# The second products of an MLP by one level of Strassen's scheme, on one Trainium2 core

## What is computed

```python
hm = rms_norm(x, g_mlp[l])
x = x + jnp.square(jax.nn.relu(hm @ w_up[l])) @ w_down[l]   # w_up 1024 x 4096, w_down 4096 x 1024
return rms_norm(x, g_final)
```

## Time and profile before

| | |
|---|---|
| median of 3 runs (lowest, highest) | 1576.56 us (1574.56, 1578.52) |
| the profiled execution | 1579.46 us |
| its span in the trace | 1577.7 us |
| busy: PE, DVE, ACT, POOL | 1531.7, 890.2, 715.3, 223.5 us |
| the MLP, from about 1219 us to the end | about 358 us |

### The profile page before, as it was taken

The page is one execution under the profiler, slowest core; times in us unless marked ns, Lnnn a source line. Parts: engine busy times, 40 slices in busy tenths (PEclk is TensorE's granted clock), DMA queues, the critical chain, the costliest instruction groups (busy, mean ns, idle before and its releaser), DMA issues.

```text
span 1577.7 us, 19176 instructions
## 1 busy us (share of the span) xinstructions
PE 1531.7 (97%) x7086; PEld 1239.6 (79%) x7086; DVE 890.2 (56%) x1753; ACT 715.3 (45%) x1630; POOL 223.5 (14%) x194
## 2 busy tenths in 40 slices
PE   7998999999999999999899999999999999999998
PEld 5886777877898777777587878788777888888886
DVE  6467485657565566666457557664455444434344
ACT  6553343334355667665335354442344433324243
POOL 3203020202120003122022005220001100000001
PEclk9999999999999999999999999999999999999999
DMA  6522121323424221112133312134323333333332
GB/s 194 161 68 80 54 80 55 107 68 120 119 76 147 77 61 56 54 56 67 41 121 94 94 55 67 56 109 131 93 81 94 94 93 96 105 94 93 97 103 81
DMA packets 88636, 141.56 MB, mean 90 GB/s; under 512 B 6368, under 2 KB 36448, under 8 KB 88544
## 3 DMA queue, kind: packets, MB, share of 16 engines
q1 hardware_dynamic: 87824, 139.55, 29.3%
q10 hardware_dynamic: 720, 0.80, 0.2%
HBM read 138.23 MB, written 2.10 MB: 89 GB/s over the span
## 4 chain that ended last, share of the span: by engine, by line
PE 79%; DVE 8%; ACT 5%; issue 3%; POOL 3%; DMA 2%; SPq 0%; ACTq 0%; POOLq 0%; DVEq 0%
PE banks L1259 12%; PE banks L1261 12%; PE banks L1260 12%; PE banks L1264 10%; PE banks L1266 10%; PE banks L1265 10%; PE banks L1222 3%; DVE sb_w_split L1964 3%; ACT sb_junk L1529 2%; DVE sb_arena L1973 2%; PE banks L1437 1%; PE banks L1384 1%; ACT sb_w_split L1561 1%; PE banks L1500 1%; DVE sb_arena L1964 1%
## 5 line engine op out<-in xcount | busy, mean ns | idle before, releaser
L1964 DVE TENSOR_TENSOR sb_w_split<-sb_raw,sb_w_split 128x512 fp32r<-128x512 f32 (+4 forms) x530 | 345.0, 693 | 365.9 <-ACT sb_w_split L1561 365.5
L1561 ACT ACTIVATE sb_w_split<-sb_raw 128x512 fp32r<-128x512 f32 (+4 forms) x530 | 288.1, 592 | 411.2 <-PE banks L1261 192.0
L1259 PE MATMUL banks<-sb_actA,sb_w_split 128*128 128x512 f32 x672 | 277.1, 412 | 2.8 <-DVE sb_arena L1964 2.5
L1261 PE MATMUL banks<-sb_actA,sb_w_split 128*128 128x512 f32 x672 | 263.0, 391 | 0.0
L1260 PE MATMUL banks<-sb_actA,sb_w_split 128*128 128x512 f32 x672 | 262.1, 390 | 0.0
L1264 PE MATMUL banks<-sb_w_split,sb_actB 128*128 128x512 f32 (+2 forms) x464 | 181.4, 391 | 1.6 <-DVE sb_w_split L1964 1.6
L1266 PE MATMUL banks<-sb_w_split,sb_actB 128*128 128x512 f32 (+2 forms) x464 | 175.9, 379 | 0.0
L1265 PE MATMUL banks<-sb_w_split,sb_actB 128*128 128x512 f32 (+2 forms) x464 | 175.5, 378 | 0.0
L1264 PE MATMUL banks<-sb_w_split,sb_actA 128*128 128x512 f32 (+1 forms) x384 | 154.4, 402 | 13.5 <-DVE sb_w_split L1964 9.6
L1259 PEld LDWEIGHTS banks<-sb_actA,sb_w_split 128*128 128x128 f32 x672 | 126.5, 188 | 32.7 <-issue 7.1
L1266 PE MATMUL banks<-sb_w_split,sb_actA 128*128 128x512 f32 (+1 forms) x384 | 150.3, 391 | 0.0
(11 more groups left out here) (226 smaller groups left out, 2188.2 us busy)
## 6 DMA issues: line engine op xcount, KB each, us to landing
sb_raw<-in_a_w_in SPq DMA_DIRECT2D x66, 256.0 KB, 3.0
sb_raw<-in_w_up SPq DMA_DIRECT2D x32, 512.0 KB, 3.8
sb_raw<-in_w_down SPq DMA_DIRECT2D x32, 512.0 KB, 3.8
sb_raw<-in_w_in SPq DMA_DIRECT2D x24, 512.0 KB, 3.7
sb_raw<-in_mem_w_kv SPq DMA_DIRECT2D x16, 512.0 KB, 3.8
sb_raw<-in_w_ckv SPq DMA_DIRECT2D x16, 512.0 KB, 3.8
sb_raw<-in_a_w_in SPq DMA_DIRECT2D x15, 512.0 KB, 3.7
sb_raw<-in_a_w_out SPq DMA_DIRECT2D x12, 512.0 KB, 3.9
```

The lines of the kernel that those rows point to most:

```text
L1259: pe.op.matmul(out, hi[:, cs], x.hi(k), start=i == 0, stop=False)
L1261: t = pe.op.matmul(out, lo[:, cs], x.hi(k), start=False, stop=last_i)
L1561: act.op.activation(hi[:, cs], raw[:, cs], ACT.Copy).then_inc(act.mark(m("w_hi"), 2 * n + part + 1), 1)
L1964: dve.op.tensor_tensor(out, a, b, op).then_inc(dve.mark(*mark) if mark else dve.tick(), 1)
```

## The change

It replaces `dn{b}0` and `dn{b}1` of each block by seven products `wn{b}{i}` of quarter size: 512 of contraction, 256 tokens (two tiles), 512 output columns. Write the squared activations of a block as a 2 x 2 matrix of blocks f00, f01, f10, f11 (token half, feature half) and the weights as W00, W01, W10, W11. In the order of execution (`WINO_ORDER`) they are:

| product | left | weight | goes to |
|---|---|---|---|
| P1 | f00 | W00 | x, and a running sum |
| P2 | f01 | W10 | x |
| Q5 | S1 = f10 - f11 | W00 + W01 | x, twice |
| Q7 | f10 - f00 | W01 + W11 | x, twice |
| P6 | S2 = f00 - S1 | W00 + W01 + W11 | the running sum |
| Q3 | f01 - S2 | W11 | x |
| N4 | -f11 | W00 + W01 + W11 + W10 | x |

- **Weights.** The four quarters of a block (1 MB each) are loaded whole by SP (`fetchR`), two into the arena and two into `x_res`, which is free by then. The sums are made in place by DMAs that POOL issues with `accum_op=ALU.add` (`tsum`, 512 KB each, eight in a block), each after the split of the chunk that it changes. Chunks of `wn` are split from there by one ACT and one DVE instruction of 128x1024 each. A chunk of `wn` is 12 matmuls.
- **Activations.** ACT squares each tile into `f_plain`; `s1` and `ssum` make the differences on DVE; `g` makes the high part (ACT) and the low part (DVE) of each left operand, 128x512 at a time, two for each product. The relu buffer has two tiles in place of eight. `up{b}0` and `up{b}1` now take two tiles of each feature half, loaded as two DMAs of 256 KB a chunk.
- **Norm scale.** It is applied before the square: DVE's eviction of `up` is max(., 0) times `row["e"]`, which `nrow` makes (four transposes on PE, a copy on ACT). `esum` and `r2` are gone.
- **Results.** Products with two destinations are added by two DVE operations a tile; 20 a block in place of 8. After the last block `fix` adds the running sum onto three quarters of x (six DVE operations), and token tiles 0 and 1 are closed after Q3, tiles 2 and 3 after N4.
- **Banks.** The MLP rotates through all eight PSUM banks, except in the up products of block 0.

The core of the diff:

```diff
-        for half in range(2):
-            add(f"dn{b}{half}", ("w_down",), D_MODEL, [(half * 512, 512)], "token", f"f{b}", "tok", k0=b * D_MODEL)
+        for i in range(7):
+            add(f"wn{b}{i}", None, 512, [(0, 512)], "token", f"F{b}{i}", "wn" if len(LANDS[i]) == 1 else "wn2",
+                tokens=SEQ // 2)
...
+        p.soon.extend([[("g", b, P1, 0), ("g", b, P2, 0)], [("s1", b, 0)], [("g", b, Q5, 0)], [("ssum", b, 3, 0), ("g", b, N4, 0)],
+                       [("g", b, Q7, 0)], [("ssum", b, 2, 0)], [("g", b, P6, 0), ("ssum", b, 4, 0)], [("g", b, Q3, 0)]])
+        p.product(f"up{b}1", into=banks(4) if b else (0, 1, 2, 3),
+                  tail=lambda j: [("relu", b, up_tile(1, j))] + ([("g", b, P1, 1)] if j == 1 else []))
...
+        work = {P1: [[("g", b, P2, 1), ("tsum", b, Q5, 0)], [("s1", b, 1), ("g", b, Q5, 1), ("tsum", b, Q5, 1)]],
+                P2: [[("tsum", b, P6, 0)], [("ssum", b, 3, 1), ("tsum", b, P6, 1)]],
+                Q5: [[("g", b, Q7, 1)], [("ssum", b, 2, 1)]], Q7: [[("g", b, P6, 1)], [("ssum", b, 4, 1)]],
+                P6: [[("g", b, Q3, 1), ("tsum", b, N4, 0)], [("g", b, N4, 1), ("tsum", b, N4, 1)]], Q3: [], N4: []}
...
+        if b == 3:
+            work[Q3] = [[("fix", 0)], [("fix", 1)], [("fix", 2)],
+                        [(kind, *([1] if kind == "fsq" else []), j) for j in (2, 3) for kind in ("fsq", "fg")]]
...
             if is_wino(name):
+                dve.wait_ge(m("w_hi"), 2 * n + 2)
+                dve.op.tensor_tensor(lo, raw, hi.bitcast(F32), ALU.subtract
+                                     ).then_inc(dve.mark(m("w_lo"), 2 * n + 2), 2)
+                continue
...
+        elif kind == "tsum":
...
+            pool.op.dma_start(v.wino_weight(i, c), v.io["w_down"][r0:r0 + 256, c0:c0 + 512].rearrange("(k p) n -> p k n", p=P),
+                              accum_op=ALU.add).then_inc(m(f"dma_sum{i}{c}"), 16)
```

More of the change, by code:

```diff
@@ L408, in need, with product @@
                 self.force(step)
-    def product(self, name, before_ev=(), soon=None, into=None, first=True, tail=None):
+    def product(self, name, before_ev=(), soon=None, into=None, first=True, tail=None, whole=False):
         pr = PRODUCTS[name]
@@ L415, in product @@
         ks, i, n_j = k_tiles(name), 0, n_out(name)
-        spans = [(c,) for c in range(len(pr.order))] if tail is None else [(0,), tuple(range(1, len(pr.order)))]
+        spans = [tuple(range(len(pr.order)))] if whole else [(c,) for c in range(len(pr.order))]
         for span in spans:
@@ L778, in order_of_work @@
     p.put(("load_g",))
-    p.side(0, [("sqp", "e", 7)], lag=0)
-    p.side(0, (), ("nsq", "e"), ("esum",), lag=4000)
+    scales(0, "e", after=[("sqp", "e", 7)])
     for j in range(TT):
         for g in range(2):
-            p.side(0, (), ("xt", j, g))
-    for b in range(4):
[L785 to L789, removed]
+            p.side(0, (), ("xt", j, g), lag=1300)
@@ L997, in __init__ @@
         at = Layout(self.arena)
-        self.out_sb = at.take(TT, D_MODEL)
-        self.relu, self.sq = at.take(KD, SEQ), at.take(2, SEQ)
+        at.at = 4096
+        flat = self.x_res[:, :, :].rearrange("p a b -> p (a b)")
+        first = Layout(self.arena).take(2, 4 * 512)
+        self.w_quarter = [w.rearrange("p (k n) -> p k n", k=4) for w in
+                          (first[:, 0, :], first[:, 1, :], flat[:, 0:2048], flat[:, 2048:4096])]
+        self.f_plain, self.relu = at.take(KD, SEQ), at.take(2, SEQ)
         at.at = 9280
         self.x_tok, self.g_row = at.take(TT, D_MODEL), at.take(D_MODEL)
+        self.out_tile = [a[:, i, :] for a in (flat[:, 0:2048].rearrange("p (a b) -> p a b", a=2),
+                                              first[:, 1, :].rearrange("p (a b) -> p a b", a=2)) for i in range(2)]
+        self.first_sum = at.take(2, 512)
+        at.at = 19520
+        self.s_plain = at.take(2, 512)
+        self.row["e"] = at.take(SEQ)
         def squares_at(ring, total, n=2):
@@ L1174, in raw_total, with wino_split @@
     def raw_total(self, n):
-        return 16 * sum(len(PRODUCTS[self.plan.chunks[m][0]].parts) for m in range(n % RAW_SLOTS, n + 1, RAW_SLOTS))
+        return 16 * sum(len(PRODUCTS[self.plan.chunks[m][0]].parts) for m in range(n % RAW_SLOTS, n + 1, RAW_SLOTS)
+                        if not is_wino(self.plan.chunks[m][0]))
+    def wino_split(self, b, i, c):
+        return self("w_lo"), 2 * self.plan.chunk_of[f"wn{b}{i}", c] + 2
 class Stream:
@@ L1611, in scalar_program @@
             j = a[0]
-            half = v.out_sb[:, j, 0:512]
+            early = 512 * (j // 2)
+            half = v.out_tile[j][:, early:early + 512]
             act.wait_ge(*m.at("f_g", ("fg", j)))
@@ L2658, in sync_program @@
             sp.wait_ge(*m.at("out_a", ("fin", j)))
-            sp.op.dma_start(io["out"][j * P:(j + 1) * P, :], v.out_sb[:, j, :]).then_inc(m("dma_out"), 16)
+            sp.op.dma_start(io["out"][j * P:(j + 1) * P, :], v.out_tile[j]).then_inc(m("dma_out"), 16)
+        elif kind == "fetchR":
+            b, i = a
+            if b == 0 and i >= 2:
+                sp.wait_ge(*m.emptied(("xt", TT - 1, 1)))
+                sp.wait_ge(*m.at("t_lo", ("turn", "hE", KD - 1)))
+                sp.wait_ge(*m.at("sq", ("sqa", "e", KD - 1)))
+            elif b:
+                for c in range(2):
+                    sp.wait_ge(*m.wino_split(b - 1, (N4, Q7, P2, Q3)[i], c))
+            r0, c0 = b * D_MODEL + 512 * (i // 2), 512 * (i % 2)
+            sp.op.dma_start(v.w_quarter[i], io["w_down"][r0:r0 + 512, c0:c0 + 512].rearrange("(k p) n -> p k n", p=P)
+                            ).then_inc(m(f"dma_quarter{i}"), 16)
         elif kind == "load_g":
```

217 lines of the change are left out of this document (174 added, 43 removed).

## The result

Median 1600.22 us (1596.25 to 1602.19), before 1576.64 (1574.56 to 1578.52): ratio 1.0146, 95% interval 1.013 to 1.0162. The kernel is slower by 23.6 us. The prediction had it slower by 10.5: the sign holds, the size is less than half of what came. The profiled execution took 1602.19 us, its span is 1600.1 us, 22.4 over the span of before.

What follows compares the result with a forecast made beforehand. PE, busy 97%, was taken to bound the kernel. 1579.5 - 21.8 + 0.4 + 14.0 + 2.6 + 15.3 = 1590.0, 10.5 over the profiled execution; on the median 1576.6 that gives 1587 us, 8-in-10 range 1571 to 1602.

Steps and rivals of the forecast that it cites:

- What is removed, what DVE must do: Seven-product blocks: 96 fewer matmuls save 21.8 us on PE; DVE has 35.5 us of work in 38.1.
- The handover: From up products to P1, P2, Q5: late splits make PE wait 4.7 us a block, 14.0 for three blocks.
- Keep up: Rival at the handover: DVE and ACT keep up, PE never waits, only the closings' chain remains; 1565 us, chance 0.14.
- half of it: Rival: 2.3 us lost a block, no low clock, closings starting 3 us earlier; 1574 us, chance 0.14.
- The clock: Behind the handover's waits: one low-clock stretch in each block, 0.85 us net each, 2.6 us in all.
- The closings: End of the last block: four closings in a row on DVE, 3.15 us each; that block loses 15.3 us in all.
- Costs that I put at nothing: Accumulating DMAs, fetchR and raw up chunks: hidden, 0 us; a sum lands after 6 us with 7.6 free for P6.
- Slow sums: Rival at P6 and N4: sums land after 10 us, 1.6 us lost at each, 13 in all; 1600 us, chance 0.13.
- POOL's DMAs take DVE's time: Rival where DVE is full: five of eight sums cost it 1.1 us each, 22 in all; 1609 us, chance 0.09.
- The rule that the prediction weighed: DVE and GpSimd share a port pair; by it a block's eight sums neither hold DVE nor are held, sum stays 1587.

Runs made afterwards that it cites:

- e5: e3 with P2's first weight split moved ahead of the squares of the last two up tiles at the handover; 1580.62 us, ratio 1.0026.
- e9: e7 with Q5's second activation split later, weight splits between evictions, row-tile work spread, last two gain products on VectorE; forecast 1565 us, measured 1572.46, ratio 0.9968.
- e11: e9 with Q5's first weight split moved ahead of both evictions of P1; 1573.5 us, ratio 0.9978.
- e8: The changed kernel, descriptor room still 1024 bytes, with only the handover order of e5; 1592.66 us, ratio 1.0106.
- e10: e9 with the room for POOL's DMA descriptors left at 1024 bytes a partition; 1583.77 us, ratio 1.0045.
- e1: The changed kernel without the 32 accumulating DMAs, weights used as single quarters, so its output differs; 1583.77 us, ratio 1.0048.
- e3: The changed kernel with 2048 instead of 1024 bytes a partition for POOL's DMA descriptors, and a bf16 scratch output; 1585.09 us, ratio 1.0055.
- e7: e3 with the handover order of e5 and a reordered end, each closing cut in two steps; 1577.74 us, ratio 1.0009.

## Why the prediction was right and wrong

- **What is removed, what DVE must do: right.** 672 matmuls in place of 768 in the second products, one each 0.2267 us. DVE operations as sized: 0.605 to the next, 1.22 for 128x1024; ACT's wide split 1.06 for 1.15. Only `fetchR` was under-sized: the quarters landed after 8.3 and 13.4 us (medians of the two kinds) for 6.9, but no wait of PE comes from it.
- **The handover: right, to 13%.** 0.31, 1.80, 1.38 and 0.62 us at the places named, for 0.3, 2.0, 1.5 and 0.85: 4.1 a block for 4.7, 16.4 in all. "Keep up" and "half of it" fall with it. e5, e9 and e11 add that it isn't one late split: behind it stand others, and a stretch of some 10 us in which DVE has no pause.
- **The clock: wrong in its place.** The 2.6 us were put behind the handover. Its waits of 1.8 and 1.4 us, 2.7 us of matmuls between them, left the granted clock at 1.00 in every block. It fell behind the 2.45 and 2.51 us waits of P6 (and in e8 and e10 behind 3.4 and 3.65), two stretches, 3.2 us. In the sum it looks right, by luck (2.6 for 3.2); as a mechanism it belongs to the sums: without them (e1) the MLP has no low clock at all.
- **The closings: right, a little large.** In a row on DVE, 3.2 apart, 4.2 in the middle, as the walk had it. The last block loses 4.1 at the handover, 1.9 within (e1), 7.0 at the end: 13.0 for 15.3.
- **The failed step is "Costs that I put at nothing": the accumulating DMAs.** The landing was right (5.8 for 6). P6's first sum too: issued 15.7 us after the up products' end, forecast 15.5. What failed is that I gave each sum its own 7.6 us and asked nothing of the second. A product's second chunk comes due 2.7 us behind the first, but POOL could not issue its sum until the first had landed: 6.0 to 6.3 us apart. In block 1 Q5's second split is done by 1375.9, its sum starts at 1380.61. That makes 12 us from the first issue to the second landing where I had about 8. The term put at 0 costs 16.5 us by the medians (e1), 15.1 of which are the room for descriptors (e3); by the MLP's stretch it costs 13.4 and 12.5. That is the better figure: the waits that go with the sums (28.7 - 18.3 us) and the low clock (3.2) make 13.6. The stretch grew by 20.8: 13.4 for the sums and 7.4 for all the rest, for which the forecast had 10.5.
- **"Slow sums" gave the right time, 1600, for the wrong reason.** It had each sum land after 10 us. Only Q7's first sums in blocks 1 to 3 do (9.7, 9.8, 10.9 us, beside SP's loads), and PE doesn't wait for them; those of P6 and N4 land after 5.7 to 6.0. That the stated range reached to 1600 at all is owed to this rival. It is a good warning of how little a time says on a cause: e1 alone would have borne it out; POOL's timeline, the landings and e3 do not.
- **"POOL's DMAs take DVE's time": refuted.** A wide split on DVE up to 1520 us takes 1219 ns in e3, whose 28 sums start beside it, and 1220 in e1, which has none:

```profile
L2142 DVE TENSOR_TENSOR sb_w_split<-sb_arena,sb_w_split 128x1024 fp32r<-128x1024 f32 x32 | 39.0, 1219 | 7.8 <-ACT sb_w_split L1670 7.8
```

```profile
L2142 DVE TENSOR_TENSOR sb_w_split<-sb_arena,sb_w_split 128x1024 fp32r<-128x1024 f32 x32 | 39.0, 1220 | 22.8 <-ACT sb_w_split L1670 22.8
```

  The rule that the prediction weighed, the Trainium skill, SBUF — State Buffer, section "SBUF: two separate sides", agrees for DMAs. What does hold DVE is an operation of POOL that reads SBUF, as in the earlier trace rows and at the end of e7.
- **Left open in part: why e9 is 7.5 us above its expectation.** Of the 13 us looked for, its waits give 4.3 (7.8 for e7's 12.1) and the end 0.7. The end is held by something new: the four stores now run at once. The window (columns as before) has the DMA engines full, at 400 GB/s, and 5.7 us follow the start of the last scaling where 3.9 did:

```profile
1566.00:1569.00 3.00, 0.00 (x0) 0.00 (x0) 0.00 (x0) 0.00 (x0) 0.00 (x0) 0.50 1.01 400
```

## What to carry to other kernels

A transfer has two prices: when it lands, and how soon the next can be issued. For DMAs of GpSimd the second can be set by the room for descriptors, which a kernel short of SBUF cuts first; look whether an issue that waits for nothing follows the landing of the one before, and try half the size or twice the room. When two runs differ by a few us, compare the stretch that was changed, not only the whole. When work is taken off a full engine, follow the engines that feed it through the first 10 us of each stage, and when a late split is moved up, name what then stands last: twice here it was the next split.
